# The delta-rule block inverse of a fused encoder layer: four of its levels in compact 32x32 blocks

## What is computed

```python
kb = kc * bc[..., None]
lower = einsum('bhid,bhjd->bhij', kb, kc) * decay * strict
rhs = concatenate([vc * bc[..., None], kb * exp(g_cum)[..., None]], axis=-1)
sol = triangular_solve(eye + lower, rhs, left_side=True, lower=True, unit_diagonal=True)
```

## Time and profile before

| | us |
|---|---|
| median of 3 runs | 2898.8 (2898.03 to 2899.04) |
| the profiled execution, its own time | 2898.46 |
| its span in the trace | 2896.9 |
| PE busy in the span | 2858.2 (99%) |
| PEld busy | 2388.9 (82%) |
| DVE busy | 1634.9 (56%) |
| ACT busy | 1051.3 (36%) |
| POOL busy | 443.3 (15%) |

### The profile page before, as it was taken

How to read it: one execution, slowest core, us unless ns; L and a number is a source line. 1 busy time by engine, 2 the same in 40 slices (tenths; PEclk the granted TensorE clock), 3 DMA queues, 4 the chain that set the end, 5 groups by cost and what they waited for, 6 DMA issues and landing times.

```text
span 2896.9 us, 36961 instructions
## 1 busy us (share of the span) xinstructions
PE 2858.2 (99%) x14208; PEld 2388.9 (82%) x14208; DVE 1634.9 (56%) x1592; ACT 1051.3 (36%) x1139; POOL 443.3 (15%) x453
## 2 busy tenths in 40 slices
PE   8999999999999999999999999999999999999997
PEld 5877888878889988899888888888888888888886
DVE  7434666655454443534434434334334798888888
ACT  5323343432454332433434332322322333333334
POOL 2000222200001123200011223323323200000001
PEclk9999999999999999999999999999999999999999
DMA  5333222222347764423322555655655855555555
GB/s 167 93 81 90 73 62 66 76 76 77 113 118 218 229 219 123 163 88 128 120 102 73 164 178 172 193 177 170 195 177 173 298 217 213 207 217 207 213 206 134
DMA packets 453633, 439.58 MB, mean 152 GB/s; under 512 B 9104, under 2 KB 365488, under 8 KB 453424
## 3 DMA queue, kind: packets, MB, share of 16 engines
q1 hardware_dynamic: 424288, 344.56, 38.6%
q0 software_dynamic: 29264, 93.90, 9.1%
HBM read 360.31 MB, written 75.50 MB: 150 GB/s over the span
## 4 chain that ended last, share of the span: by engine, by line
PE 89%; DVE 3%; issue 2%; ACT 2%; POOL 2%; DMA 1%; SPq 0%; DVEq 0%; POOLq 0%; ACTq 0%
PE slab_ps L843 18%; PE slab_ps L845 18%; PE slab_ps L844 18%; PE down_ps L1398 6%; PE down_ps L1400 6%; PE down_ps L1399 6%; PE mix_ps L845 2%; PE mix_ps L844 2%; PE mix_ps L843 2%; PE down_ps L843 2%; PE down_ps L844 2%; PE down_ps L845 2%; POOL dn_ctt L675 1%; PE mix_ps L892 1%; PE mix_ps L899 1%
## 5 line engine op out<-in xcount | busy, mean ns | idle before, releaser
L843 PE MATMUL slab_ps<-act_hi,w_hi 128*128 128x512 f32 (+2 forms) x2704 | 1023.5, 379 | 13.5 <-DVE act_lo L2069 11.0
L845 PE MATMUL slab_ps<-act_hi,w_lo 128*128 128x512 f32 (+2 forms) x2704 | 1000.6, 370 | 0.0
L844 PE MATMUL slab_ps<-act_lo,w_hi 128*128 128x512 f32 (+2 forms) x2704 | 999.6, 370 | 0.0
L2017 DVE TENSOR_TENSOR w_lo<-w_raw,w_hi 128x2048 fp32r<-128x2048 f32 x200 | 469.5, 2347 | 370.5 <-ACT w_hi L1424 369.7
L843 PEld LDWEIGHTS slab_ps<-act_hi,w_hi 128*128 128x128 f32 (+1 forms) x2704 | 509.7, 188 | 107.4 <-issue 22.8
L845 PEld LDWEIGHTS slab_ps<-act_hi,w_lo 128*128 128x128 f32 (+1 forms) x2704 | 509.2, 188 | 88.0 <-issue 0.8
L844 PEld LDWEIGHTS slab_ps<-act_lo,w_hi 128*128 128x128 f32 (+1 forms) x2704 | 509.9, 189 | 86.8 <-issue 6.3
L1424 ACT ACTIVATE w_hi<-w_raw 128x2048 fp32r<-128x2048 f32 x200 | 382.0, 1910 | 522.0 <-PE slab_ps L845 400.5
L1398 PE MATMUL down_ps<-half_hi,u_slot 128*128 128x512 f32 x896 | 349.5, 390 | 0.8 <-DVE half_lo L2701 0.8
L1400 PE MATMUL down_ps<-half_lo,u_slot 128*128 128x512 f32 x896 | 349.5, 390 | 0.0
L1399 PE MATMUL down_ps<-half_hi,u_slot 128*128 128x512 f32 x896 | 349.4, 390 | 0.0
(11 more groups left out here) (378 smaller groups left out, 3124.9 us busy)
## 6 DMA issues: line engine op xcount, KB each, us to landing
w_raw<-in_w_mlp_up_dram SPq DMA_DIRECT2D x64, 1024.0 KB, 6.5
b<-in_w_mlp_down_dram SPq DMA_DIRECT2D x64, 1024.0 KB, 6.8
w_raw<-in_w_in_dram SPq DMA_DIRECT2D x56, 1024.0 KB, 5.6
u_slot<-u_park SPq DMA_DIRECT2D x112, 512.0 KB, 8.2
w_raw<-in_w_cross_kv_dram SPq DMA_DIRECT2D x32, 1024.0 KB, 6.2
u_park<-u_hi POOLq DMA_DIRECT2D x32, 896.0 KB, 9.1
u_park<-u_lo POOLq DMA_DIRECT2D x32, 896.0 KB, 8.9
w_raw<-in_w_mix_out_dram SPq DMA_DIRECT2D x16, 1024.0 KB, 5.9
```

What stands on the lines that cost most here:

```text
L843: mm(ps, wh, xh, start=first, stop=False)
L844: mm(ps, wh, xl, start=False, stop=False)
L845: return mm(ps, wl, xh, start=False, stop=last)
L2017: tt(w_lo[:, slot], w_raw[:, slot], f32(w_hi[:, slot]), ALU.subtract).then_inc(on["slab_lo"], 1)
```

## The change

For levels 0 to 4 (blocks up to 32) nothing crosses a 32x32 diagonal block. The change keeps these 16 diagonal blocks of a head compact: partitions 32g to 32g+31 hold diagonal block g of each of the four token tiles, so that a whole head is 128 partitions x 4 x 32 elements.

- **Setup.** POOL copies the diagonal blocks of five level masks and of the identity into `blk_mask` and `blk_ident` (24 copies, once, with `blk_u` cleared behind them).
- **Start of a head.** DVE copies the diagonal blocks of `dn_lt` into `blk_l` (4 copies), makes level 0 in `blk_x`, identity minus it in `blk_xt`, four masked products in `blk_c` (levels 1 to 4), and transposes 128x128 in place of 128x512.
- **Levels 1 to 4.** U and V are 16 products of 32x32 by 32x16 each (4 token tiles x 4 blocks) instead of 4 products of 128x128 by 128x64. Block g uses rows and columns 32g to 32g+31 of the array. All 16 write the same PSUM bank, block g its own 32 partitions. ACT copies and DVE subtracts 64 elements a partition instead of 256.
- **Behind level 4.** DVE transposes three blocks into `dn_xx` and copies four into `dn_xt`, on the diagonal of matrices that POOL has cleared.
- **POOL.** Two masked products a head (levels 5 and 6) instead of seven, three clears (`dn_xt`, `dn_xx`, `dn_uu`) instead of five, then the mask of `dn_at`, all at once behind `dn_lt`.
- **PE's places.** Each wait moves one place ahead of its products, with one group of slab products between. Level 1: wait for the inverse at place 10, U at 11, wait at 12, V at 13. The second window: waits at 1, 3, 6, 8, 10, 12, products at 2, 4, 7, 9, 11, 13. Level 5 begins at place 1 of the third, as before.

Core of the diff:

```diff
+            for g in range(NB):
+                r = block_rows(g)
+                for n in range(5):
+                    chain.put(nc.gpsimd.tensor_copy(blk_mask[r, n], lvl_mask[r, 6 - n, r]))
+                chain.put(nc.gpsimd.tensor_copy(blk_ident[r], ident[r, r]))
+            chain.sync()
+            nc.gpsimd.memset(blk_u[:], 0.0).then_inc(on["consts"], 1)
...
                     pool.wait_ge(on["dn_pair"], hd + 1)
-                    for n in range(7):
-                        if n == 2:
-
-                            pool.wait_ge(on["dn_at"], hd + 1)
-                            nc.gpsimd.tensor_tensor(flat3(dn_at[:]), flat3(dn_at[:]), every_tile(tri_incl[:]),
-                                                    ALU.mult).then_inc(on["dn_masked"], 1)
...
+                    for n in (5, 6):
+                        nc.gpsimd.tensor_tensor(flat3(dn_ctt[:, n % 2]), flat3(dn_lt[:]), every_tile(lvl_mask[:, 6 - n]),
                                                 ALU.mult).then_inc(on["dn_ct"], 1)
-                        if n == 0 or n >= 3:
-                            nc.gpsimd.memset(dn_uu[:], 0.0).then_inc(on["dn_zero"], 1)
+                    for t in (dn_xt, dn_xx, dn_uu):
+                        nc.gpsimd.memset(t[:], 0.0).then_inc(on["dn_zero"], 1)
+                    pool.wait_ge(on["dn_at"], hd + 1)
+                    nc.gpsimd.tensor_tensor(flat3(dn_at[:]), flat3(dn_at[:]), every_tile(tri_incl[:]),
+                                            ALU.mult).then_inc(on["dn_masked"], 1)
...
-                for _ in range(7):
+                for _ in range(6):
                     yield HOP
 
-                for n in range(1, 7):
-                    pe.wait_ge(on["dn_ct"], hd * 7 + (n + 1))
+                for n in range(1, 5):
+                    pe.wait_ge(on["dn_x"], hd * 7 + n)
+                    yield HOP
+                    for c in range(NT):
+                        for g in range(NB):
+                            r = block_rows(g)
+                            last = mm(halves_of(M[2][r, c * BK:(c + 1) * BK], n, 0), blk_c[r, n - 1, c],
+                                      halves_of(blk_x[r, c], n, 0), start=True, stop=True)
+                    last.then_inc(on["dn_u"], 1)
+                    yield HOP
+                    pe.wait_ge(on["dn_uev"], hd * 6 + n)
+                    yield HOP
+                    for c in range(NT):
+                        for g in range(NB):
+                            r = block_rows(g)
+                            last = mm(halves_of(M[4][r, c * BK:(c + 1) * BK], n, 1), blk_u[r, n - 1, c],
+                                      halves_of(blk_xt[r, c], n, 1), start=True, stop=True)
+                    last.then_inc(on["dn_v"], 1)
+                    if n in (1, 4):
+                        yield SEG
+                    else:
+                        for _ in range(4 - n):
+                            yield HOP
+
+                for n in range(5, 7):
+                    pe.wait_ge(on["dn_ct"], hd * 2 + (n - 4))
                     pe.wait_ge(on["dn_x"], hd * 7 + n)
...
-                dve.wait_ge(on["dn_ct"], hd * 7 + 1)
-                chain.link(tt(flat3(dn_xt[:]), every_tile(ident[:]), flat3(dn_ctt[:, 0]), ALU.subtract))
-                v.transpose(dn_xx[:], dn_xt[:]).then_inc(on["dn_x"], 1)
+                for g in range(NB):
+                    chain.put(v.tensor_copy(blk_l[block_rows(g)], diagonal(dn_lt, g)))
+                chain.sync()
+                over = lambda m: m.unsqueeze(1).broadcast_to([P, NT, BK])
+                chain.link(tt(blk_x[:], blk_l[:], over(blk_mask[:, 0]), ALU.mult))
+                chain.link(tt(blk_xt[:], over(blk_ident[:]), blk_x[:], ALU.subtract))
+                for n in range(4):
+                    tt(blk_c[:, n], blk_l[:], over(blk_mask[:, n + 1]), ALU.mult)
+                v.transpose(flat(blk_x), flat(blk_xt)).then_inc(on["dn_x"], 1)
...
+                def take_block_v(n):
+                    dve.wait_ge(on["dn_x"], hd * 7 + n)
+                    dve.wait_ge(on["dn_v"], hd * 6 + n)
+                    xt = halves_of(flat(blk_xt), n, 1)
+                    chain.link(tt(xt, xt, halves_of(M[4][:, 0:NT * BK], n, 1), ALU.subtract))
+                    if n < 4:
+                        v.transpose(flat(blk_x), flat(blk_xt)).then_inc(on["dn_x"], 1)
+                        return
+                    dve.wait_ge(on["dn_zero"], hd * 3 + 2)
+                    for g in range(NB - 1):
+                        chain.put(v.transpose(diagonal(dn_xx, g), blk_xt[block_rows(g)]))
+                    for g in range(NB):
+                        last = v.tensor_copy(diagonal(dn_xt, g), blk_xt[block_rows(g)])
+                        if g < NB - 1:
+                            chain.put(last)
+                    chain.sync()
+                    last.then_inc(on["dn_x"], 1)
```

More of the change, by code:

```diff
@@ L161, in build @@
     BETA, DECAY = 32, 64
+    BK, NB = 32, P // 32
     SMALL = DECAY + NH
@@ L267, in build @@
         lvl_mask = sb("lvl_mask", [P, 7, P])
+        blk_mask = sb("blk_mask", [P, 5, BK])
+        blk_ident = sb("blk_ident", [P, BK])
+        blk_u = sb("blk_u", [P, 4, NT, BK])
         with ExitStack() as scope:
@@ L306, in build @@
             dn_kdec = sb("dn_kdec", [P, S])
+            blk_l = sb("blk_l", [P, NT, BK])
+            blk_x = sb("blk_x", [P, NT, BK])
+            blk_xt = sb("blk_xt", [P, NT, BK])
             dn_st = sb("dn_st", [P, P])
@@ L398, in build, with block_rows, diagonal @@
         flat3 = lambda t: t.rearrange("p (t s) -> p t s", s=P)
+        flat = lambda t: t[:].rearrange("p c s -> p (c s)")
         per_tile = lambda c: c.unsqueeze(2).broadcast_to([P, NT, P])
         every_tile = lambda m: m.unsqueeze(1).broadcast_to([P, NT, P])
+        def block_rows(g):
+            return slice(g * BK, (g + 1) * BK)
+        def diagonal(t, g):
+            return flat3(t[block_rows(g)])[:, :, block_rows(g)]
         def packed(t, j):
@@ L1574, in take_u @@
                     act.wait_ge(on["dn_u"], hd * 6 + n)
-                    if n < 6:
-                        act.wait_ge(on["dn_zero"], hd * 5 + n)
-                    fn(halves_of(dn_uu[:], n, 0), halves_of(M[2][:], n, 0), ACT.Copy).then_inc(on["dn_uev"], 1)
+                    if n == 5:
+                        act.wait_ge(on["dn_zero"], hd * 3 + 3)
+                    u = blk_u[:, n - 1].rearrange("p c s -> p (c s)") if n < 5 else dn_uu[:]
+                    ps = M[2][:, 0:NT * BK] if n < 5 else M[2][:]
+                    fn(halves_of(u, n, 0), halves_of(ps, n, 0), ACT.Copy).then_inc(on["dn_uev"], 1)
                 take_u(1)
@@ L2186, in delta_first @@
                 yield HOP
+                dve.wait_ge(on["consts"], 3)
                 chain.link(v.memset(dn_rows[:].bitcast(F32), 0.0))
@@ L2246, in take_v @@
                     xt = halves_of(dn_xt[:], n, 1)[rows]
-                    last = tt(xt, xt, halves_of(M[4][:], n, 1)[rows], ALU.subtract)
-                    if n < 5:
-                        chain.link(last)
-                        last = v.transpose(dn_xx[:], dn_xt[:])
-                    last.then_inc(on["dn_x"], 1)
+                    tt(xt, xt, halves_of(M[4][:], n, 1)[rows], ALU.subtract).then_inc(on["dn_x"], 1)
                 yield SEG
-                take_v(1)
+                take_block_v(1)
                 yield HOP
@@ L2260, in delta @@
                 for t in range(2):
-                    take_v(t + 2)
+                    take_block_v(t + 2)
                     delta_conv(1 - par, hd + 1, t)
                 yield SEG
-                take_v(4)
+                take_block_v(4)
                 delta_silu(hd + 1, (0, 1))
```

12 lines of the change are left out of this document (3 added, 9 removed).

## The result

The changed kernel took **2915.49 us** (median of 5 runs, 2915.09 to 2916.31) beside 2899.04 for the kernel before (5 runs, 2898.03 to 2900.87). The ratio is 1.0057, 95% interval 1.0047 to 1.0068: slower, by 16.5 us. The forecast was 2902.6 in a range of 2890 to 2918. The profiled execution has a span of 2913.9 us at a mean granted clock of 0.993 (before: 2896.9 and 0.998), so the two spans differ by 17.0 us.

A forecast was written before the change was run, and what follows sets the result against it. PE's queue was taken to bound the kernel (busy 99%). Terms -8.0 - 2.8 + 13.2 + 1.2 + 0.4 = +4.0 us on 2898.46 gave a forecast of 2902.6 us, range 2890 to 2918.

The forecast's parts named there:

- the case that I called likeliest: Whole kernel: PE's work traded for PE's waiting, +4.0 us to 2902.6, own range 2898 to 2908, chance 0.45.
- PE's products: U and V of levels 1 to 4: 32 product groups at 0.65 us instead of 0.90, -8.0 us.
- Rival 1: Quarters sharing a PSUM bank work in one file: 1.32 us a group, +21.4, so 2924; chance 0.14.
- POOL's waits at levels 3 and 4: PE's waits for POOL's mask products, 0.3 and 0.41 us in each of four heads, go: -2.8 us.
- The head's start: PE's wait for each head's first inverse grows by 3.3 us, as DVE's copies meet POOL's work: +13.2 us.
- My model of the first inverse: DVE's instructions take turns one for one with POOL's clears and mask; transpose done at 381.55, 2.9 us later.
- Rival 2: DVE isn't held by POOL's clears and mask: a head starts +1.7 instead of +3.3 us, total 2896; chance 0.20.
- Behind level 4: PE's wait before level 5 for DVE's eviction, subtraction, transposes and copies: 0 to 0.6, taken as 0.3; +1.2 us.
- Set-up: POOL's 24 setup copies and a clear, beside DVE's sums that PE waits for: +0.4 us (0 to 1).
- The clock: Rival: PE's long stands make its clock fall, about half of 5 us each; 2905 to 2913, said 2908; chance 0.10.
- one gap with an unchanged pace: In the trace of before, a PE gap of 2.7 us left the pace of the products as it was.
- What I said would show it: Timeline signs: groups 0.60 to 0.70 us, 3 to 4 us stands released by `blk_x`, heads about 68.3; wrong above 70.

The follow-up runs named there:

- e2: The changed kernel with DVE making the blocks directly behind `dn_lt`, ahead of `dn_at` and the scalings, POOL as it was: 2903.58 us (one run).
- e1: The changed kernel with POOL's first masks and clears waiting until the first inverse is made: 2895.28 us, ratio 0.9989 to the kernel before.
- e3: The changed kernel with both DVE's order of e2 and POOL's wait of e1: 2889.27 us, ratio 0.9967 to the kernel before.
- e6: e3 with PE's loop over pairs of delta heads written out: 2887.89 us (one run).
- e4: The kernel before with five linked transposes added ahead of each head's first inverse, no 32x32 product: 2923.35 us (one run).
- e8: e3 with the four products of one block together instead of the four blocks of one tile: 2899.85 us (one run).

## Why the prediction was wrong in its likeliest case

The range held the result and "slower" was among its cases, but the case that I called likeliest, +4 us without a fall of the clock, did not happen. Step by step:

- **PE's products, forecast -8.0, measured -10.6.** The mechanism was right, and so were its parts: 8 x 0.032 for four quarters at once and 0.31 around them make the 0.57 measured, where I had 8 x 0.030 and 0.36, and then rounded their 0.60 up to 0.65. Rival 1, one file at 1.32 a group, is refuted. The Trainium skill's rule, in TensorEngine Tiling (Array Packing), section Restrictions and Gotchas, that different row tiles can't access the same PSUM bank at the same time, did not have the effect that I had drawn from it. Whether it is broken here no run shows: by a slab product's pace (0.227 us for 512 columns) a product of 16 columns takes an estimated 0.007 us, and that is how far apart the four quarters start. So their products may well have written one after the other, with only the loads and the rest of the 0.032 us side by side.
- **POOL's waits at levels 3 and 4, forecast -2.8, measured -2.9.** They are gone, and the 1.04 us from start to start that I had taken for a product without a wait is what the timeline of before shows.
- **The head's start, forecast +13.2, measured +15.1.** The cause was right. My model of the first inverse had it done at 381.55; it was done at 385.84, which in the time of before (3.91 earlier, by the start of POOL's first mask) is 381.93. The model's detail was not right: POOL doesn't take turns one for one with a copy of DVE, it goes first, and the copy gets in only ahead of a mask or when POOL has finished. Here the two give almost the same sum, and that is luck: in e2 one copy stands for 2.61 us, which turns would not give. Rival 2 (no hold at all, 2896) is what e1 made true by its edit, at 2895.3. That the totals agree is luck too: the rival had +6.8 for the heads' starts and e1's waits are only 3.1 above those of before, while level 5, the loop and a new wait before level 3 cost more than it had.
- **Behind level 4, forecast +1.2, measured +2.4**, a wait for DVE's last copy of 0.4 to 0.6 us where I took 0.3, inside the 0 to 0.6 that I had named, and 0.1 more in the product behind each.
- **Set-up, forecast +0.4, measured 0.** The first head starts at 299.86 in place of 300.02.
- **The clock, nothing in my sum and a rival of 0.10, measured +11.1. This is the step that failed.** I had every piece of it: a stand of 3.7 us, in the first head 4.9, the pace of 0.42 after idleness, and a price of about 2.5 for each fall, which came out at 2.7 to 2.9 in this kernel. What I had against it was one gap with an unchanged pace: one draw from what e3 and e6 show to be an open throw at that length, and it says nothing about 4 us. I also centred the rival at 2908, between one and four falls, when my own four stands were all of a length at which every trace here has the clock fall (3.2 us and more, 9 of 9). Four falls put on my sum make 2902.6 + 11.1 = 2913.7; of the remaining 1.8 the other terms' errors (-2.6, -0.1, +1.9, +1.2, -0.4) and the next point (+1.3) make 1.3, and half a microsecond is not placed.
- **Unforeseen: +1.3 at PE's backward jump.** I costed nothing there; e6 shows that the stand goes with the loop.

What I said would show it, showed it: the group (0.57, just below the 0.60 to 0.70 that I gave), the stand released by `blk_x`, POOL in no wait of levels 2 to 4. The heads, at 70.6 to 72.8 us, were past the 70 above which I called myself wrong.

## What to carry to other kernels

A wait on the engine that bounds the kernel has a second price: past some 2 us it may, and from 2.7 us on here it always did, bring work at half clock behind it that costs 1.5 to 1.7 us more where the clock is down for 3.4 us and 2.7 to 3.0 where it is down for 6.8, so look at the granted clock in the windows behind each new stand and not at the busy share. When work is moved to VectorE, look at what GpSimd does in that very stretch; here one changed semaphore wait, without one instruction fewer, was worth 20 us. And put small products so that neighbours in the queue lie on different quarters of the array: the same group took 0.57 us in place of 1.02.

## What the runs showed of the hardware that I had not expected

- GpSimd's instructions, back to back, held a VectorE copy with one input and 128 elements a partition for 1.46 us in place of 0.22, and in e2 for 2.61. A copy got through where a mask of GpSimd's came next or nothing did, never where a clear came next, in all eight heads of the two kernels. GpSimd's own durations hardly changed (0.52 for a clear, 1.26 to 1.32 for a mask). Why a mask lets it in was not tried.
- The granted clock fell after some stands of 2.1 us and not after others of the same length in the same execution, and after the same gap at 285 us in some executions of an unchanged stretch and not in others. This makes 1.7 to 2 us of the spread between runs. In two traces it fell where PE had not stood at all. It was down for 3.4 us or for 6.8, and equal stands (3.62, 3.63 and 3.65 in e4) had either.
- 32x32 pairs of load and product went at 0.032 us a pair on one quarter and at four pairs every 0.032 us on four, although all wrote to one PSUM bank. With a quarter's eight pairs in a row (e8) neighbouring quarters overlapped only in part: 0.70 us from first to last start against 0.26.
- A backward jump of PE's loop cost 0.9 to 1.5 us between two heads in the kernels with the small products and nothing visible at that place before. Whether the number of instructions in the loop's body is what matters was not tried.
